# Second norm of an encoder step: the split rows of tiles 0 to 5 lie over columns that the output projection's last group no longer reads

## The reference, cut to what matters

```
h = rmsnorm(x, norm_mix_w) * (1 + sc_m) + sh_m
mix = [SSD heads | differential attention](h @ w_in) @ w_out
x = x + g_m * mix                                        # x2 in the kernel
h = rmsnorm(x, norm_ffn_w) * (1 + sc_f) + sh_f           # the second norm
u = causal_dwconv(h @ w_up)                              # width 3, 2 * 2816 columns
x = x + g_f * ((silu(gate) * val) @ w_down)
y = rmsnorm(x, final_norm_w)
```

## Time and profile before

| | |
|---|---|
| runs (us) | 1784.60, 1776.79, 1783.99 |
| profiled execution, its own time | 1778.84 us |
| its span, first to last instruction | 1777.1 us |
| its mean granted TensorE clock | 0.960 |
| output projection | 769 to 901 us |
| up-projection of tiles 0 to 5 | 910 to 1278 us |
| down-projection and up-projection of tiles 6 to 8 | 1279 to 1761 us |

### The profile page before, as it was taken

The page is one execution under the profiler, slowest core; times in us unless marked ns, Lnnn a source line. Parts: engine busy times, 40 slices in busy tenths (PEclk is TensorE's granted clock), DMA queues, the critical chain, the costliest instruction groups (busy, mean ns, idle before and its releaser), DMA issues.

```text
span 1777.1 us, 23446 instructions
## 1 busy us (share of the span) xinstructions
PE 1639.3 (92%) x9297; PEld 1449.5 (82%) x9297; DVE 994.3 (56%) x1567; ACT 640.5 (36%) x1155; POOL 447.2 (25%) x261
## 2 busy tenths in 40 slices
PE   5799998699998987798979999999999999999996
PEld 4688896589995665576779999999989889989875
DVE  3765318642115664444567666666547677667744
ACT  4522123211113553353333222222544454444532
POOL 0121124231210000045564333333351122112132
PEclk8899999899997998999989999999999999999998
DMA  9555110231213002736632222222264435444452
GB/s 335 164 165 181 36 27 1 54 85 36 76 61 124 1 1 72 237 108 177 230 101 74 70 60 63 69 60 87 68 182 131 138 107 154 134 163 119 142 166 69
DMA packets 164562, 192.25 MB, mean 108 GB/s; under 512 B 7858, under 2 KB 126875, under 8 KB 164416
## 3 DMA queue, kind: packets, MB, share of 16 engines
q1 hardware_dynamic: 139626, 132.11, 24.3%
q10 hardware_dynamic: 19612, 40.93, 7.2%
q0 software_dynamic: 5216, 17.71, 2.9%
HBM read 173.62 MB, written 17.11 MB: 107 GB/s over the span
## 4 chain that ended last, share of the span: by engine, by line
PE 50%; DVE 5%; DMA 3%; POOL 2%; ACT 1%; issue 1%; ACTq 0%; DVEq 0%
PE PS L628 10%; PE PS L629 10%; PE PS L630 10%; PE PS L1077 5%; PE PS L1078 5%; PE PS L1079 5%; PE PS L551 1%; DMA k_cache<-in_cache_k_dram 1%; PE PS L1006 1%; PE PS L1007 1%; PE PS L1008 1%; DMA x_rows<-x_scratch 1%; POOL h_lo L2290 1%; DVE y_new L1579 1%; DVE y_tmp L1585 1%
## 5 line engine op out<-in xcount | busy, mean ns | idle before, releaser
L2277 POOL TENSOR_TENSOR weights_lo<-weights_raw,weights_hi 128x1024 fp32r<-128x1024 f32 x103 | 268.7, 2609 | 792.3 <-ACT weights_hi L1789 792.2
L628 PE MATMUL PS<-h_hi,weights_hi 128*128 128x384 f32 x1280 | 435.9, 341 | 11.0 <-POOL h_lo L2290 7.8
L629 PE MATMUL PS<-h_lo,weights_hi 128*128 128x384 f32 x1280 | 433.2, 338 | 0.0
L630 PE MATMUL PS<-h_hi,weights_lo 128*128 128x384 f32 x1280 | 433.0, 338 | 0.0
L1789 ACT ACTIVATE weights_hi<-weights_raw 128x1024 fp32r<-128x1024 f32 x202 | 213.6, 1058 | 166.7 <-PE PS L1079 100.1
L628 PEld LDWEIGHTS PS<-h_hi,weights_hi 128*128 128x128 f32 x1280 | 243.2, 190 | 20.2 <-issue 19.8
L629 PEld LDWEIGHTS PS<-h_lo,weights_hi 128*128 128x128 f32 x1280 | 243.2, 190 | 0.0
L630 PEld LDWEIGHTS PS<-h_hi,weights_lo 128*128 128x128 f32 x1280 | 243.0, 190 | 0.0
L2404 POOL TENSOR_TENSOR g_lo<-g_T,g_hi 128x384 fp32r<-128x384 f32 x66 | 84.7, 1284 | 343.5 <-ACT g_hi L2164 343.5
L1077 PE MATMUL PS<-weights_hi,g_hi 128*128 128x512 f32 x396 | 160.2, 405 | 8.7 <-POOL g_lo L2404 5.2
L1078 PE MATMUL PS<-weights_lo,g_hi 128*128 128x512 f32 x396 | 159.0, 401 | 0.0
(11 more groups left out here) (385 smaller groups left out, 2518.3 us busy)
## 6 DMA issues: line engine op xcount, KB each, us to landing
weights_raw<-in_w_up_dram SPq DMA_DIRECT2D x88, 512.0 KB, 4.0
weights_raw<-in_w_down_dram SPq DMA_DIRECT2D x66, 512.0 KB, 4.4
w_ada_unit<-in_w_ada_dram SPq DMA_DIRECT2D x32, 512.0 KB, 5.6
weights_raw<-in_w_in_dram SPq DMA_DIRECT2D x24, 512.0 KB, 5.3
weights_raw<-in_w_out_dram SPq DMA_DIRECT2D x24, 512.0 KB, 3.8
w_ada<-in_w_ada_dram SPq DMA_DIRECT2D x4, 2048.0 KB, 20.9
k_cache<-in_cache_k_dram ACTq DMA_DIRECT2D x8, 1024.0 KB, 5.5
x_rows<-x_scratch ACTq DMA_DIRECT2D x9, 512.0 KB, 4.3
```

The lines of the kernel that those rows point to most:

```text
L628: pe.matmul(out, wh, xh, start=(i == 0), stop=False)
L629: pe.matmul(out, wh, xl, start=False, stop=False)
L630: mm = pe.matmul(out, wl, xh, start=False, stop=(i == n - 1))
L2277: mark(gp.tensor_tensor(WL[n % 3][:, :], WR[:, n % 3, :], WH[n % 3][:, :].bitcast(F32), ALU.subtract), "w_lo")
```

## The change

`h2_hi` and `h2_lo` keep the layout of `YH` and `YL` (rows of 1152 columns) and lie right over them, in columns 0 to 767, which belong to the groups 0 and 1 and which group 2 no longer reads. So each tile is split inside group 2: `h2_split(f - 2)` and `norm_tile(0, f - 2)` stand at units f = 2 to 7, and the tiles are turned one unit earlier (`OUT_NORM_AT`). The statistics and the division read tiles 0 to 5 where `gate_and_add` left them (`X2_ROWS`), not from the scratch: tiles 0 to 2 get their statistics in group 1, tiles 3 to 5 in group 2. The load of the third group's rows of x into `XA` moves from unit 4 to unit 5 and waits until VectorE has normed the tile that lay there. The first two groups of the up-projection go to banks 6 and 7 (`up_bank`). Buffers of the up-projection move: `val`, `gate`, `gate_silu` and the last four tiles of `g_T` lie in the columns 768 to 1151 beside `h2_hi` and `h2_lo`, as two pieces of 384 each, with 1152 from one piece to the next. The tail rows of the convolution lie in two places, and are stored by four transfers where there were two. The scratch is still written.

```
     NA = 768
-    FH = r("h2_hi", [P, KT, NA], F32R)
-    FL = r("h2_lo", [P, KT, NA], F32R)
-    GT = r("g_T", [P, FT, NA])
+    HALVES_NA = NA // TG
+    FH = [at("h2_hi", [P, KT, T], R2, F32R)]
+    FL = [at("h2_lo", [P, KT, T], R1, F32R)]
+    beside_hi = at("beside_h2_hi", [P, KT, T], R2)
+    beside_lo = at("beside_h2_lo", [P, KT, T], R1)
+    GT = [at(f"g_T{f}", [P, HALVES_NA, TG], R1 + KT * T * 4 + f * NA * 4)[:, :, :] for f in range(12)] + \
+         [at(f"g_T{f}", [P, HALVES_NA, TG], R3 + (f - 12) * NA * 4)[:, :, :] for f in range(12, 18)] + \
+         [beside_lo[:, 2 * i:2 * i + 2, NA:T] for i in range(4)]
+    CV = [[beside_hi[:, 2 * i:2 * i + 2, NA:T] for i in range(2)]]
+    CG = [beside_hi[:, 4:6, NA:T]]
+    CGS = [beside_hi[:, 6:8, NA:T]]
...
+    UV = [at("up_val", [P, 2, NA + 2], ff), r("up_val_b", [P, 2, NU2])]
+    UG = [at("up_gate", [P, 2, NA + 2], ff + (2 * (NA + 2) * 4 + 31) // 32 * 32), r("up_gate_b", [P, 2, NU2])]
...
-    N2R = [[at(f"h2_raw{i}", [P, KT, P], off)
-            for i, off in enumerate((R4, R4 + 4096, r.off, r.off + 4096, R3, gh_off))]]
...
+    N2 = at("x2_normed", [P, 2, D], ff)
+    N2J = at("x2_squares_unread", [P, D], R1 + KT * T * 4 + 4096)
+    N2R = [[at(f"h2_raw{i}", [P, KT, P], R3 + 4096 * i if i < 4 else ff + 8192 + 4096 * (i - 4)) for i in range(6)]]
+    X2_ROWS = XM[0] + XM[1]
...
+    YA = r("y_new", [P, 3, D])
+    N2R.append([h2_raw_b[:, jj % 2, :, :] for jj in range(3)])
+    FH.append(at("h2_hi_b", [P, KT, T], R1, F32R)[:, :, 0:TG])
+    FL.append(at("h2_lo_b", [P, KT, T], R1, F32R)[:, :, TG:2 * TG])
+    tail_a = at("ffn_tail_rows_a", [18, KT, T], R1)
+    FROWS = [tail_a[:, q, 0:512] for q in range(8)] + [tail_b[:, q, :] for q in range(3)]
...
-        OUT_NORM_AT = [2, 3, 4, 5, 6, 7]
+        OUT_NORM_AT = [1, 2, 3, 4, 5, 6]
+
+        def up_bank(i):
+
+            return (i + 6) % 8
...
-                elif i >= 6:
+                elif i < 2:
                     pe.wait_ge(sem("h_raw"), 2 * 6)
                 else:
-                    pe.wait_ge(sem("mix_out"), 12 + i + 1)
-                up_group(N_FFN0 + u, 0, i, i % 8, g)
+                    pe.wait_ge(sem("mix_out"), 12 + up_bank(i) + 1)
+                up_group(N_FFN0 + u, 0, i, up_bank(i), g)
...
-                    mark(ve.tensor_scalar(N2[:, jj % 2, :], XR[:, jj % 2, :], STAT[:, 16 + jj:17 + jj], None, ALU.mult),
+                    mark(ve.tensor_scalar(N2[:, jj % 2, :], X2_ROWS[jj], STAT[:, 16 + jj:17 + jj], None, ALU.mult),
                          "normed")
...
-                    return (buf[:, shift:shift + NA],)
+                    return (buf[:, shift:shift + NA].rearrange("p (a n) -> p a n", a=HALVES_NA),)
...
-                LP, n = (NA, NA) if grp == 0 else (256, TG)
+                into = (dst,) if grp == 0 else (dst[:, 0:256], dst[:, 256:TG].rearrange("p (b t) -> p b t", b=NB))
                 for t in range(3 - grp):
                     w = FFNC[:, c, t:t + 1]
-                    for part, src in enumerate(parts(grp, buf, t)):
-                        d = dst[:, 0:LP] if part == 0 else dst[:, LP:n].rearrange("p (b t) -> p b t", b=NB)
+                    for d, src in zip(into, parts(grp, buf, t)):
...
-                out(ve.tensor_tensor(GT[:, f, 0:n], CV[grp][:, f % 2, 0:n], CGS[grp][:, 0:n], ALU.mult), "gated")
+                out(ve.tensor_tensor(GT[f][:, 0, :] if grp else GT[f], CV[grp][f % 2], CGS[grp], ALU.mult), "gated")
...
-            def x2_fetch(jj):
-                if jj >= 3:
-                    ac.wait_ge(sem(f"rows_out{jj - 3}"), 16)
-                load(XR[:, jj % 2, :], x2_d[jj * P:(jj + 1) * P, :], f"xr_in{jj % 2}")
-
             def x2_stats(jj):
-                ac.wait_ge(sem(f"xr_in{jj % 2}"), dma_count[f"xr_in{jj % 2}"])
-                if jj >= 2:
-                    ac.wait_ge(sem("h_turned"), 2 * (jj - 1))
-                ch(ac.activation(N2[:, jj % 2, :], XR[:, jj % 2, :], ACT.Square, accum_out=STAT[:, 48 + jj:49 + jj]))
+                ac.wait_ge(sem("x_new"), 2 * (jj + 1))
+                ch(ac.activation(N2J[:, :], X2_ROWS[jj], ACT.Square, accum_out=STAT[:, 48 + jj:49 + jj]))
                 mark(ac.activation(STAT[:, jj:jj + 1], STAT[:, 48 + jj:49 + jj], ACT.Sqrt, bias=C("eps"), scale=1.0 / D),
                      "h_sd")
-                if jj >= 1:
-                    ac.wait_ge(sem("normed"), jj)
-                    if jj + 1 < 6:
-                        x2_fetch(jj + 1)
...
-                    if (g, f) in ((0, 5), (2, 4)):
+                    if (g, f) in ((0, 5), (2, 5)):
                         for jj in range(3):
                             if g == 0:
                                 ac.wait_ge(sem(f"rows_in{jj}"), 16)
                             else:
                                 ac.wait_ge(sem(f"rows_out{jj}"), 16)
+                                ac.wait_ge(sem("normed"), 3 + jj + 1)
                             load(XA[:, jj, :], x_all[3 * (1 + g // 2) + jj], f"rows_in{jj}")
-                    if (g, f) == (2, 0):
-                        ac.wait_ge(sem("first_rows_out"), 48)
-                        x2_fetch(0)
-                        x2_fetch(1)
-                        ac.wait_ge(*once("ffn_turned"))
-                    elif g == 2 and f <= 6:
-                        x2_stats(f - 1)
+                    if g == 1 and 3 <= f < 6:
+                        x2_stats(f - 3)
+                    if g == 2 and f < 3:
+                        x2_stats(3 + f)
+                    if g == 2 and f >= 2:
+                        h2_split(f - 2)
...
-            ac.wait_ge(sem("out_used"), 3 * KT)
-            for jj in range(6):
-                h2_split(jj)
...
+                    ac.wait_ge(sem("first_rows_out"), 48)
...
+                if i == 0:
+                    ac.wait_ge(sem("h_lo"), 6)
+                mark(ac.activation(U[:, 2 + g * TG:2 + (g + 1) * TG], PS[:, up_bank(i), 0:TG], ACT.Copy), "up_out")
...
-            for jj in range(6):
-                norm_tile(0, jj, N2R[0], FH[0], FL[0])
+                    if g == 2 and f >= 2:
+                        norm_tile(0, f - 2, N2R[0], FH[0], FL[0])
...
-            store(o["ffn_conv_prompt"][0, 0], FROWS[0:2, :], "ftail_stored")
-            store(o["ffn_conv_sample"][0].rearrange("b t c -> (b t) c"), FROWS[2:18, :], "ftail_stored")
+            for dst, r0, r1 in ((o["ffn_conv_prompt"][0, 0], 0, 2), (o["ffn_conv_sample"][0].rearrange("b t c -> (b t) c"), 2, 18)):
+                store(dst[:, 0:8 * 512].rearrange("r (q n) -> r q n", q=8), tail_a[r0:r1, :, 0:512], "ftail_stored")
+                store(dst[:, 8 * 512:].rearrange("r (q n) -> r q n", q=3), tail_b[r0:r1, :, :], "ftail_stored")
```

More of the change, by code:

```diff
@@ L269, in build @@
     FROW = at("ffn_conv_rows", [20, 2 * DFF], R4)
-    r = Region(KEEP_END, top)
     NA = 768
-    FH = r("h2_hi", [P, KT, NA], F32R)
-    FL = r("h2_lo", [P, KT, NA], F32R)
-    GT = r("g_T", [P, FT, NA])
+    HALVES_NA = NA // TG
[6 more added lines that the diff above has]
+         [beside_lo[:, 2 * i:2 * i + 2, NA:T] for i in range(4)]
@@ L276, in build @@
+    CV = [[beside_hi[:, 2 * i:2 * i + 2, NA:T] for i in range(2)]]
+    CG = [beside_hi[:, 4:6, NA:T]]
+    CGS = [beside_hi[:, 6:8, NA:T]]
+    r = Region(R4, top)
     FFNC = r("ffn_conv_cols", [P, 2 * FT, 20])
     FTAIL = r("ffn_conv_tails", [P, 2 * FT, 2 + 2 * NB])
-    gh_off = r.off
+    ff = r.off
+    NU2 = 2 + 256 + NB * (TS + 2)
+    UV = [at("up_val", [P, 2, NA + 2], ff), r("up_val_b", [P, 2, NU2])]
+    UG = [at("up_gate", [P, 2, NA + 2], ff + (2 * (NA + 2) * 4 + 31) // 32 * 32), r("up_gate_b", [P, 2, NU2])]
@@ L279, in build @@
+    val_b = r("val_b", [P, 2, TG])
+    CV.append([val_b[:, i, :] for i in range(2)])
+    CG.append(r("gate_b", [P, TG])[:, :])
+    CGS.append(r("gate_silu_b", [P, TG])[:, :])
+    assert r.off >= ff + 4 * (NA + 2) * 4 + 32
+    SQJ = at("squares_unread", [P, D], r.off)
     GH = [r(f"g_hi{i}", [P, TG], F32R) for i in range(2)]
     GL = [r(f"g_lo{i}", [P, TG], F32R) for i in range(2)]
[L281 to L284, removed]
@@ L285, in build @@
-    CG = r("gate", [P, NA])
-    CGS = r("gate_silu", [P, NA])
-    SQJ = at("squares_unread", [P, D], ff - 4 * TG * 4)
-    YSQR = XR[:, 0, :]
[L290 to L299, removed]
@@ L301, in build @@
-    N2R = [[at(f"h2_raw{i}", [P, KT, P], off)
-            for i, off in enumerate((R4, R4 + 4096, r.off, r.off + 4096, R3, gh_off))]]
-    r = Region(KEEP_END, KEEP_END + 2 * KT * NA * 4)
+    YSQR = XR[:, 0, :]
+    N2 = at("x2_normed", [P, 2, D], ff)
+    N2J = at("x2_squares_unread", [P, D], R1 + KT * T * 4 + 4096)
+    N2R = [[at(f"h2_raw{i}", [P, KT, P], R3 + 4096 * i if i < 4 else ff + 8192 + 4096 * (i - 4)) for i in range(6)]]
+    X2_ROWS = XM[0] + XM[1]
+    r = Region(R2, R3)
     FNW = r("final_norm_rows", [P, D])
@@ L305, in build @@
     FGS = r("gate_ffn_sample", [P, D])
[L306 to L310, removed]
     FG = r("gate_ffn", [P, D])
     YT_ = r("y_tmp2", [P, 2, 512])
```

(23 more changed lines are left out.)

1 line of the change is left out of this document (removed).

## The result

Five executions of the changed kernel took 1758.75 to 1767.59 us, median 1764.12; five of the kernel before 1776.79 to 1784.60, median 1781.84. The ratio is 0.9905, 95% interval 0.9876 to 0.9934: some 17 us less, between 12 and 22. The profiled execution has a span of 1762.3 us against 1777.1, that is 14.8 less. The forecast was 1767.5 us, between 1759 and 1778.

What follows compares the result with a forecast made beforehand. The start of the up-projection was taken to bound the kernel, held by splits after scratch loads. 14.42 - 0.35 - 0.5 = 13.6 us gained, under a mean of 1781.06, gave 1767.5 us, range 1759 to 1778.

Steps and rivals of the forecast that it cites:

- The three losses: TensorE around the projection's end: 3.24 us idle inside the third group, 7.82 behind it, 2.84 from low clock and short wait.
- TensorE's own timetable: Projection's third group: six units of 4.20 us and six turns of 0.88; third up group at 906.35, 14.42 us earlier.
- The two costs I took off: Losses from the new order in the projection's third group: 0.35 us at tile 0's turn, 0.5 for VectorE's round per tile.
- Tile 0's turn: Now behind unit 1: VectorE's division held by GpSimd's low part, turn some 0.35 us late, ends 0 and 0.76.
- VectorE's rounds: Raw tile, division and wait for GpSimd per tile: 5.1 us with the middle wait, against TensorE's 5.08; cost taken 0.5 us.
- GpSimd's queue: Six low parts of tiles and six of weights, to 903.6; smallest cover 3.6 us, so the moved subtractions cost nothing.
- ScalarE's wait at unit 5: Loads into `XA` wait until tile 5 is divided; GpSimd 0 to 3.2 us late, inside the cover; cost nothing, end 3.2.
- The rule that speaks against it: Shared SBUF ports promise no turn: GpSimd's next instruction could take them again before VectorE, and the gain would be lost.
- The rival built on being passed over: VectorE starved in group 2: each division waits through two GpSimd instructions, 7.0 us lost, 1788 us; chance 0.05.
- Two-piece operands: Up-projection's VectorE instructions on split buffers: taken as nothing; each of 154 could grow by 0.83 us before it shows.

Runs made afterwards that it cites:

- r2: Changed kernel with the six splits of tiles 0 to 5 behind the projection again; ratio to the kernel before 0.9984 (0.9964 to 1.0005).
- r7: Changed kernel with the load of the third group's rows at unit 6 instead of 5; one run, projection's third group to third up group 49.78 us.
- r4: Changed kernel with each low part of tiles 0 to 5 computed twice by GpSimd; ratio to the kernel before 0.9996 (0.9972 to 1.0020).
- r1: Changed kernel once more, no edit; ratio to the kernel before 0.9905 (0.9882 to 0.9928).
- r3: Changed kernel, but tiles 0 to 5 loaded back from the scratch instead of read in place, splits still early; ratio to the kernel before 1.0012.
- r5: As r3, but each split one unit later; ratio to the kernel before 0.9959 (0.9935 to 0.9983).
- r6: Changed kernel with the up groups on banks 0 to 7 in order as before; one run, projection's third group to third up group 48.83 us.

## Why the prediction was right

**The three losses.** The sum was 13.90 us, 14.42 by TensorE's own timetable, and 13.6 after costs; the distance shortened by 14.22. Idle time and the gap came out as read from the earlier trace rows, and r2 brings the gap and the low clock back together.

**The timetable.** A unit with a turn was put at 5.08 us. The six turns of the changed kernel start at 868.17, 873.30 and so on to 893.60: 5.13 once, then (893.60 - 873.30) / 4 = 5.08 each. The first up product was put 39.95 us behind the third group's first product; it came at 39.30.

**The two costs I took off,** 0.35 and 0.5 us, were too high: without them the timetable gives 39.10 us, so all costs together came to 0.20. Tile 0's turn was held by VectorE's division (2.41 us, since it began inside GpSimd's instruction), as said, but only by about 0.15: it starts 0.38 us behind the start of the last product ahead of it (867.79), the next turn 0.23. VectorE's rounds cost nothing: a division finishes a whole round ahead of its turn, so the wait for GpSimd fills time in which VectorE would have waited for the next turn.

**GpSimd's queue** had 1.9 us of cover left, where I put 3.6 less up to 3.2 for ScalarE's wait at unit 5. That wait took 4.10 us and made a gap of 2.16 on GpSimd; r7 shows that it costs no time. r4 shows that the cover is as thin as that: its last low part ends 14.52 us later, counted from the third group's first product (60.25 against 45.73), and the third up group starts 12.68 later. The last two instructions took 2.89 and 2.86 us instead of 2.4, with additions of VectorE beside them, which took 2.00 to 2.10 us instead of 0.68.

**The rule that speaks against it.** *The Trainium skill, SBUF — State Buffer, section "SBUF: two separate sides", says that VectorE and GpSimd share a pair of ports as an exclusive lock: whichever starts first has it for the whole instruction, and the other fully blocks.* The traces agree with the hold (an addition in the earlier trace rows and the division of 2.41 us here both end about 0.55 us behind GpSimd's instruction: 860.25 against 859.70, 868.11 against 867.56). No run shows VectorE passed over: in r4, with GpSimd without gaps, its divisions got in after one instruction each. The rival built on being passed over, 1788 us, is out.

**Two-piece operands** cost nothing, as taken. The convolution steps on `gate` in the changed kernel (the trace calls it `beside_h_hi`), against 1893 ns in the earlier trace rows; the other forms on two pieces differ by 2 ns at most:

```profile
L1652 DVE SCALAR_TENSOR_TENSOR beside_h_hi<-up_gate,ffn_conv_cols,beside_h_hi 128x768 f32<-128x768 f32 x44 | 83.3, 1892 | 1.5
```

**What was off.** The forecast of 1767.5 us is 3.4 above the median. 0.6 of it are the costs above. The span shrank by 14.8, which is 0.6 more than the distance; the down-projection's products stretch over 480.7 us after and 481.9 before, but over the ten profiled executions that length goes from 478.4 (r7) to 481.9 whatever the edit, so this is not clearly the change's. The remaining 2.2 lie in the base: I put the 13.6 under a mean of four executions (1781.06), and the two profiled ones, 1778.84 and 1764.12, differ by 14.7. By the medians the gain is 17.7, and the interval, 12 to 22, holds both; the kernel before alone spans 14 us over its 25 executions beside r1 to r4. That the time of the runs came so near is in part luck. The distance is not: it repeats within 0.02 us (r1).

What isn't settled: why the third group's first product starts anywhere between 855.0 and 862.7 us in these executions. Nearly all of that is there at the projection's first product (765.0 to 772.3), ahead of everything the edits touch, and it was not tried.

## What to carry to other kernels

Buffers tied to the end of a stage can hold a whole chain of work behind it; when a stage's last part reads only some columns, the next stage's operands can lie over the others, and the chain runs inside the stage. Write TensorE's own timetable first, then give each other engine's queue its due times and look at the smallest cover. And check each in-order queue for rings: an instruction that waits for another engine, with the next round's first step queued behind it (r3), cost more here (11.4 us) than the transfers that I meant to blame (3.3 us of idle time in r5).

## What the runs showed of the hardware that I had not expected

The granted clock fell without idle time, in three of the ten profiled executions. In r6 and r7 the windows of 5 us above show 0.64 to 0.68, in and behind the 44 turns of 20 x 20 (2.95 us in r6, 3.45 in r7), with TensorE busy throughout. r3 shows the same, from its third group's first product on:

```profile
859.87:864.87 5.00, 5.00 (x17) 3.97 (x16) 4.70 (x7) 0.00 (x0) 0.78 (x1) 0.66 0.74 270
```

In finer windows the clock stands at 0.50, the lower level of 1.2 GHz, in r3 from 861.87 to 863.87, in r6 from 857 to 859 and in r7 from 862.67 to 866.67. TensorE was busy without a gap in the 10 us before (851.87 to 861.87 in r3, 847 to 857 in r6, 849 to 859 in r7). In r3 and r6 it did products, then the 44 turns, then some products more, and then the clock fell; in r7 it fell within the turns (0.79 from 859.67 to 862.67). In the other seven executions, with the same instructions there, the clock was 1.00. It cost 1.2 and 2.2 us in r6 and r7, and 1.4 in r3: the first turn comes 10.95 us behind the third group's first product there and 9.51 in r5, both with 0.73 us of idle time ahead of it. Why three of ten executions show it is open.
